# A 31-tap depthwise convolution moved to TensorE as 128x32 products over four-token stacks, and attention values as column halves

## The reference

```python
for l in range(2):
    h = rmsnorm(x, g_mix[l]); p = h @ w_in[l]            # 384 | 256 | 32 | 512 | 512 columns
    q = rmsnorm(c_q) @ w_uq[l]                           # 8 heads of 64 (nope) + 32 (rope)
    kv = rmsnorm(c_kv) @ w_ukv[l]                        # 8 heads of 64 (key) + 64 (value)
    o = softmax(q k^T * scale) @ v                       # per head, 512 x 512
    u = a * sigmoid(gt)                                  # 512 channels
    u[t, ch] = b[ch] + sum_k w_dw_conv[k, ch] * u[t + k - 15, ch]     # k in 0..30
    u = silu(layernorm(u))
    x = x + concat(o, u) @ w_o[l]
    z = dwconv3(rmsnorm(x) @ w_up[l]); x = x + (silu(zg) * zv) @ w_down[l]
return rmsnorm(x, g_final)
```

## Time and profile before

| | before |
|---|---|
| median of 3 runs | 2043.75 us |
| lowest, highest | 2043.48, 2044.87 us |
| the profiled execution | 2043.99 us |
| its span (first to last record) | 2042.3 us |
| mean granted TensorE clock, share of full | 0.988 |
| TensorE busy | 1952.7 us, 96% of the span |
| VectorE busy | 1195.6 us, 59% |
| ScalarE busy | 958.1 us, 47% |
| GpSimd busy | 147.2 us, 7% |

### The profile page before, as it was taken

One profiled execution on the slowest core, in us unless ns is written; L12 is line 12 of the kernel. 1 busy time (PEld: TensorE's weight loads), 2 busy tenths in 40 slices (PEclk: granted clock), 3 DMA queues, 4 the chain that ended last, 5 costly groups with the idle time before them and its releaser, 6 DMA issues.

```text
span 2042.3 us, 25795 instructions
## 1 busy us (share of the span) xinstructions
PE 1952.7 (96%) x8419; PEld 1540.2 (75%) x8419; DVE 1195.6 (59%) x1960; ACT 958.1 (47%) x1722; POOL 147.2 (7%) x148
## 2 busy tenths in 40 slices
PE   8999989799999988999999999999999999999997
PEld 6777778578888866765678888887766578888886
DVE  4555446643343346888566666436698757656534
ACT  4655563343443333477553444334377554434432
POOL 2111000100000003220010000003120010000000
PEclk9999989899999999999999999999999999999998
DMA  4222213133332222221123333333221033333322
GB/s 136 62 64 68 70 54 104 42 94 96 98 98 94 96 78 63 62 37 37 47 83 103 98 89 106 95 96 88 67 43 42 22 95 92 92 103 93 102 94 82
DMA packets 163423, 162.44 MB, mean 80 GB/s; under 512 B 46840, under 2 KB 121550, under 8 KB 163340
## 3 DMA queue, kind: packets, MB, share of 16 engines
q1 hardware_dynamic: 163236, 161.36, 27.1%
q10 hardware_dynamic: 104, 0.03, 0.0%
HBM read 159.24 MB, written 2.10 MB: 79 GB/s over the span
## 4 chain that ended last, share of the span: by engine, by line
PE 88%; DVE 6%; ACT 3%; issue 1%; POOL 1%; DMA 0%; SPq 0%; DVEq 0%; ACTq 0%; POOLq 0%
PE bank_b L2062 15%; PE bank_b L2064 15%; PE bank_b L2063 15%; PE bank_a L2062 12%; PE bank_a L2064 12%; PE bank_a L2063 12%; PE bank_b L2353 3%; PE bank_b L2451 2%; PE bank_a L2164 1%; PE bank_a L2437 1%; DVE x_t L1338 1%; DVE arena L1341 1%; DVE w_lo L1338 1%; DVE arena L1338 1%; DVE h_lo L1341 1%
## 5 line engine op out<-in xcount | busy, mean ns | idle before, releaser
L1338 DVE TENSOR_TENSOR w_lo<-w_raw,w_hi 128x512 fp32r<-128x512 f32 (+3 forms) x621 | 428.3, 702 | 611.0 <-ACT w_hi L1053 365.4
L1053 ACT ACTIVATE w_hi<-w_raw 128x512 fp32r<-128x512 f32 (+3 forms) x396 | 233.0, 599 | 441.9 <-PE bank_b L2064 227.8
L2062 PE MATMUL bank_b<-h_hi,w_hi 128*128 128x512 f32 x944 | 371.2, 393 | 7.4 <-DVE var L1356 3.9
L2063 PE MATMUL bank_b<-h_lo,w_hi 128*128 128x512 f32 x944 | 367.9, 390 | 0.0
L2064 PE MATMUL bank_b<-h_hi,w_lo 128*128 128x512 f32 x944 | 367.8, 390 | 0.0
L2062 PE MATMUL bank_a<-h_hi,w_hi 128*128 128x512 f32 x592 | 235.2, 397 | 30.8 <-DVE h_lo L1341 16.3
L771 ACT ACTIVATE w_hi<-w_raw 128x512 fp32r<-128x512 f32 x225 | 137.8, 629 | 259.4 <-PE bank_b L2064 138.5
L1341 DVE SCALAR_TENSOR_TENSOR arena<-arena,cols_all 128x512 f32<-128x512 f32 x350 | 244.9, 750 | 0.1
L2063 PE MATMUL bank_a<-h_lo,w_hi 128*128 128x512 f32 x592 | 233.1, 394 | 0.0
L2064 PE MATMUL bank_a<-h_hi,w_lo 128*128 128x512 f32 x592 | 233.0, 394 | 0.0
L2062 PEld LDWEIGHTS bank_b<-h_hi,w_hi 128*128 128x128 f32 x944 | 177.5, 188 | 49.0 <-issue 5.0
(11 more groups left out here) (262 smaller groups left out, 2495.9 us busy)
## 6 DMA issues: line engine op xcount, KB each, us to landing
w_raw<-in_w_up_dram SPq DMA_DIRECT2D x240, 256.0 KB, 3.0
w_raw<-in_w_down_dram SPq DMA_DIRECT2D x152, 256.0 KB, 2.5
w_raw<-in_w_in_dram SPq DMA_DIRECT2D x64, 128.0 KB, 2.3
w_raw<-in_w_gate_dram SPq DMA_DIRECT2D x32, 256.0 KB, 2.9
w_raw<-in_w_in_dram SPq DMA_DIRECT2D x32, 256.0 KB, 2.6
w_raw<-in_w_o_dram SPq DMA_DIRECT2D x32, 256.0 KB, 2.6
w_raw<-in_w_out_dram SPq DMA_DIRECT2D x16, 256.0 KB, 2.6
w_raw<-in_w_in_dram SPq DMA_DIRECT2D x16, 192.0 KB, 2.3
```

The costliest lines, as they stand in the source:

```text
L1053: nc.scalar.activation(w_hi[:, s, 0:c], w_raw[:, s, 0:c], ACT.Copy).then_inc(w_round, 1)
L1338: return nc.vector.tensor_tensor(out_, a, b, op)
L2062: nc.tensor.matmul(out_, a_hi, b_hi, start=start, stop=False, skip_group_check=loose)
L2063: nc.tensor.matmul(out_, a_hi, b_lo, start=False, stop=False, skip_group_check=loose)
```

## The change

**Taps.** All 31 taps move to TensorE. A channel tile's 128 partitions are cut into four lanes of 32 channels. For lane c, `stacks[..][:, c, :]` holds on its 128 partitions four copies of the 32 channels, shifted by 0, 1, 2 and 3 tokens. It is made by `stack_up(j)`: 16 transfers within SBUF for each tile, each 32 rows of 540 fp32 numbers, issued by ScalarE. There are two such stacks, used in turn. A product of a 128x32 matrix with 512 columns of a stack then applies four taps to 32 channels, and 8 groups (`GROUPS`) of four such products, one for each lane, make up the 31 taps. The four write different quarters of the partitions of one bank. GpSimd makes the matrices, one operation for each group. `base(j)` adds the bias, and nothing is left to join. VectorE's `taps()` go.

**Values.** `vv` becomes compact (64 columns a head). `values2(j)` does one pair and one block of 128 queries: 8 products of 64 columns out over 128 moving columns, the two heads alternating, into the lower and the upper half of the partitions. It runs in every second step. The steps go through blocks first and heads second, `PV_LAG` becomes 6, and `pts` a ring of eight.

**Order.** The taps of tile 0 move from the middle of `M_KV` to the fifth `M_Q` chunk. The taps of `w_dw_conv` are loaded in 8 pieces a layer, by SyncE, in place of one.

```diff
-PE_TAPS = 8
-DVE_TAPS = CONV_K - PE_TAPS
+SHIFTS = 4
+GROUPS = -(-CONV_K // SHIFTS)
+LANES = P // SHIFTS
+STACK = S + SHIFTS * (GROUPS - 1)
-EXP_LAG, TURN_LAG, PV_LAG = 2, 4, 8
+EXP_LAG, TURN_LAG, PV_LAG = 2, 4, 6
...
@@ transfers of the taps (SyncE)
-                sp_.dma_start(rows_tap[n], w_dw_conv[n]).then_inc(rows2_land, 16)
+                for g in range(GROUPS):
...
+                    sp_.dma_start(rows_tap[n][g * rows:g * rows + rows, 0:(k1 - k0) * LANES].rearrange("q (s c) -> q s c", c=LANES),
+                                  w_dw_conv[n, k0:k1, :].rearrange("s (q c) -> q s c", c=LANES)).then_inc(rows2_land, 16)
...
@@ diagonals (GpSimd)
-                        nc.gpsimd.tensor_scalar(diag[:, r, :], ident[:, :], cols_all[:, l, c:c + 1], None,
+                        nc.gpsimd.tensor_tensor(diag[:, r, :].rearrange("p (c m) -> p c m", c=SHIFTS), taps,
+                                                lanes[:, :].unsqueeze(1).broadcast_to((P, SHIFTS, LANES)),
                                                 ALU.mult).then_inc(diag_made, 1)
...
@@ ScalarE
+                def stack_up(j):
+
+                    act.wait_ge(pad_zero, was[pad_zero.name] + 2)
+                    act.wait_ge(u_ready, was[u_ready.name] + (1, HT, HT, HT)[j])
+                    if j >= 2:
+                        act.wait_ge(diag_used, was[diag_used.name] + (j - 1) * GROUPS)
+                    for c in range(4):
+                        for s in range(SHIFTS):
+                            act.dma_start(stacks[j % 2][s * LANES:s * LANES + LANES, c, :],
+                                          upad[c * LANES:c * LANES + LANES, j, s:s + STACK]).then_inc(stack_land[j % 2], 16)
+
+                for k in range(4, 6):
                     split2(M_KV + k)
-                split2(M_Q)
-
-                act.wait_ge(diag_used, was[diag_used.name] + PE_TAPS)
-                nc.scalar.activation(conv_odd[1], conv_banks[0], ACT.Copy).then_inc(conv_base, 1)
-                for k in range(1, 4):
+                stack_up(0)
+                for k in range(6, KT):
+                    split2(M_KV + k)
+                stack_up(1)
+                for k in range(4):
                     split2(M_Q + k)
...
                 split2(M_PAIR + 1)
+                base(0)
+                stack_up(2)
                 act.wait_ge(sq_added, added0 + KT - 1 + KVT - 1)
...
                     if g == 0:
                         base(1)
+                        stack_up(3)
                         copy_key(1, 0)
...
@@ TensorE
-                def conv_taps(j, taps):
-
-                    for r in taps:
+                def conv_taps(j, groups):
+
+                    for r in groups:
                         if r == 0:
-                            pe.wait_ge(u_ready, was[u_ready.name] + j + 1)
-                            pe.wait_ge(pad_zero, was[pad_zero.name] + 2)
-                        pe.wait_ge(diag_made, was[diag_made.name] + j * PE_TAPS + r + 1)
-                        nc.tensor.matmul(conv_banks[j], diag[:, r, :], upad[:, j, DVE_TAPS + r:DVE_TAPS + r + S],
-                                         start=r == 0, stop=r == PE_TAPS - 1).then_inc(diag_used, 1)
+                            pe.wait_ge(stack_land[j % 2], stacked(l, j))
+                        pe.wait_ge(diag_made, was[diag_made.name] + j * GROUPS + r + 1)
+                        for c in range(4):
+                            rows = slice(c * LANES, c * LANES + LANES)
+                            last = nc.tensor.matmul(conv_banks[j][rows, :], diag[:, r, rows],
+                                                    stacks[j % 2][:, c, SHIFTS * r:SHIFTS * r + S],
+                                                    start=r == 0, stop=r == GROUPS - 1)
+                        last.then_inc(diag_used, 1)
...
-                def values2(n):
...
-                    part = nc.tensor.matmul(bank_b[:, i % 2, :], vv[:, kb, i, hd * P:hd * P + P], pts[hd][:, kb, :],
-                                            start=hd == 0 and kb == 0, stop=hd == 1 and kb == TT - 1)
...
+                def values2(j):
+
+                    i, b = j // TT, j % TT
+                    c = slice(b * P, b * P + P)
...
+                    for kb in range(TT):
+                        for hd in range(2):
+                            rows = slice(hd * ND, hd * ND + ND)
+                            last = nc.tensor.matmul(bank_b[rows, i % 2, c], vv[:, kb, i, rows],
+                                                    pts[(2 * j + hd) % len(pts)][:, kb * P:kb * P + P],
+                                                    start=kb == 0, stop=kb == TT - 1)
+                    last.then_inc(pv_done, 1)
...
-                        values2(g - PV_LAG)
+                    if g >= PV_LAG and (g - PV_LAG) % 2:
+                        values2((g - PV_LAG) // 2)
```

More of the change, by code:

```diff
@@ L316, in two_blocks @@
         gf = arena[:, 9:13, :]
-        CPAD = S + 2 * HALO
-        upad = arena_flat[:, 13 * S:13 * S + 4 * CPAD].rearrange("p (j n) -> p j n", j=4)
-        conv = arena[:, 18:22, :]
-        conv_odd = (arena[:, 22, :], arena[:, 29, :])
-        diag = arena_flat[:, 30 * S:32 * S].rearrange("p (r n) -> p r n", r=PE_TAPS)
-        vv = arena_flat[:, 5 * S:13 * S].rearrange("p (k i n) -> p k i n", k=TT, i=PAIRS)
+        CPAD = STACK + SHIFTS
+        upad0 = 13 * S + S // 4
+        upad = arena_flat[:, upad0:upad0 + 4 * CPAD].rearrange("p (j n) -> p j n", j=4)
+        conv = upad[:, :, 0:S]
+        stacks = [arena_flat[:, first:first + 4 * STACK].rearrange("p (c n) -> p c n", c=4) for first in (18 * S, 9 * S)]
+        diag = arena_flat[:, 30 * S:32 * S].rearrange("p (r n) -> p r n", r=GROUPS)
+        vv = arena_flat[:, 5 * S:9 * S].rearrange("p (k i n) -> p k i n", k=TT, i=PAIRS)
         prob = arena[:, 23:27, :]
@@ L331, in two_blocks @@
         lat_hi, lat_lo = split[:, 0:5, :], split[:, 5:10, :]
-        pts = (arena[:, 0:4, :], sq[:, :, :])
+        pts = [arena[:, n, :] for n in range(4)] + [sq[:, n, :] for n in range(4)]
         kq_hi, kq_lo = ([[h[:, 2 * q + hd, :] for hd in range(2)] for q in range(2)] for h in (h_hi, h_lo))
@@ L486, in two_blocks @@
         vv_ready = sem("vv_ready")
[L487 removed]
         pt_ready = sem("pt_ready")
         pv_done = sem("pv_done")
[L490 removed]
+        tap_zero = sem("tap_zero")
+        stack_land = [sem(f"stack_land{b}") for b in range(2)]
         diag_made = sem("diag_made")
         diag_used = sem("diag_used")
[L493 to L494 removed]
         conv_ready = sem("conv_ready")
@@ L675, in _ @@
                                          base=-P, pattern=[[1, 2 * P]], channel_multiplier=-1))
+            for c in range(P // LANES - 1):
+                made(nc.gpsimd.tensor_tensor(lanes[:, :], (lanes if c else ident)[:, 0:LANES],
+                                             ident[:, (c + 1) * LANES:(c + 2) * LANES], ALU.add))
             def add_squares(count, before_sq, before_add, before_stat):
@@ L1428, in first_normed @@
                                         ALU.mult).then_inc(xn_first, 1)
+            for rows in rows_tap:
+                nc.vector.memset(rows[P - LANES:P, P - LANES:P], 0.0).then_inc(tap_zero, 1)
             dve.wait_ge(cols_made, 1)
@@ L1810, in _ @@
                 for k in range(6, KT):
                     split2_lo(M_KV + k)
-                    taps(2)
-                split2_lo(M_Q)
-                taps(10)
-                for k in range(1, 4):
+                for k in range(4):
                     split2_lo(M_Q + k)
-                    taps(1)
                 dve.wait_ge(w_used, was[w_used.name] + M_KV + KT)
@@ L1837, in rstd_after @@
                     stt(var[:, :], bank, 1.0 / width, epsv, ALU.mult, ALU.add).then_inc(var_ready, 1)
-                    beside()
+                    if beside is not None:
+                        beside()
                     dve.wait_ge(guess_ready, number)
@@ L1906, in _ @@
                     split2_lo(M_PAIR + SLOTS + m)
-                first_taps = tap
                 for g in range(BLOCKS + TURN_LAG):
@@ L1934, in _ @@
                             split2_lo(M_PAIR + (i + 2) * SLOTS + (2, 4, 5, 6).index(m))
-                    if m == 1 and 2 <= i:
-                        dve.wait_ge(o_round, was[o_round.name] + i - 1)
-                        rest(o2_lo[:, i - 2, :], bank_b[:, i % 2, :], o2_hi[:, i - 2, :]).then_inc(o_split, 1)
-                    taps(taps_by(g, first_taps) - tap)
+                    if m == 7 and 1 <= i:
+                        dve.wait_ge(o_round, was[o_round.name] + i)
+                        rest(o2_lo[:, i - 1, :], bank_b[:, (i - 1) % 2, :], o2_hi[:, i - 1, :]).then_inc(o_split, 1)
                 dve.wait_ge(o_round, was[o_round.name] + HT)
@@ L2373, in _ @@
                         total(bank_a[:, 3, :], added0 + KT - 1 + KVT - 1)
+                    if k == 4:
+                        conv_taps(0, range(GROUPS))
```

142 lines of the change are left out of this document (45 added, 97 removed).

## The result

The changed kernel takes 2101.2 us (median of 4 runs, 2100.12 to 2102.16), the kernel before in the same session 2043.62 us: a ratio of 1.0281, 95% interval 1.0263 to 1.0299. It is slower by 57.6 us; 2075 was forecast, with a range of 2037 to 2132.

A forecast was written before the change was run, and what follows sets the result against it. TensorE, busy 96% of the span, was taken as the bound, level with VectorE and ScalarE in late attention steps. Terms -6.7 + 6.0 + 14.9 + 3.6 - 2.0 = +15.8 us a layer, 31.6 for two: 2075 us, range 2037 to 2132.

The forecast's parts named there:

- Taps on TensorE: Tap products: four 32-column products run side by side in 0.86 us, as one product did; cost 0.
- steps: Rival for the taps: quarters overlap only beside a product's second record, +22.4 us a layer, 2120 us; chance 0.17.
- no overlap: Rival for the taps: small products never run side by side, some +80 us a layer, 2235 us; chance 0.14.
- Values: Value products in attention steps: smaller products, two heads at once, save 6.7 us a layer; bounds 0 and -13.7.
- switches: TensorE entering and leaving bursts of small products: 30 uncovered switches at 0.2 us, +6.0 us a layer; bounds 0 and 10.
- The stacks: ScalarE's queue: 16 transfers a stack at 0.35 us each delay the work behind them, +14.9 us a layer.
- Clock: TensorE at half rate after long idle, counted once at the sum and half at stack 3: +3.6 us a layer.
- VectorE's relief: 184 tap operations leave VectorE, so its maxima and query work come sooner: -2.0 us a layer; bounds 0 and -5.
- SyncE's tap loads and GpSimd's diagonals: SyncE's 14 further tap loads (4.3 us) and GpSimd's one operation a group: both forecast at no cost.
- faster: Rival: without stalls at ScalarE's queue and their clock, -2.7 us a layer, 2039 us in all; chance 0.13.

The follow-up runs named there:

- the fourth experiment: Changed kernel with a tile's 32 small tap products reordered, all groups of one column quarter before the next quarter: 2163.83 us (1.0593), 62.6 above the changed kernel.
- experiment 5: Kernel before with the change of the values alone (compact values, 64 columns out, PV_LAG 6), taps as before: 2040.26 us (0.9985), beside 2043.65.
- experiment 6: Kernel before with 20 of VectorE's 23 tap operations of each channel tile left out, nothing else changed: 2035.26 us (0.9964), beside 2043.65.
- the second experiment: Changed kernel with GpSimd in place of ScalarE issuing the 16 transfers of each stack: 2038.05 us (0.9975), beside 2043.26.
- the seventh experiment: Version with GpSimd issuing the stacks, and the scaling of probabilities moved from ScalarE to VectorE: 2025.85 us (0.9916), beside 2043.65.

## Why the prediction was right, and where it was off

It was right in direction, inside its range, and right on the mechanism: ScalarE's issuing holds back what stands behind it. The size was short by almost half of the rise (31.6 forecast, 57.6 measured). By its own steps, a layer:

- **Taps on TensorE, 0.** Right. Four small products take what one took, 0.86 us to the next group. The two rivals against it, steps (2120) and no overlap (2235), fell, and the fourth experiment shows what there is to lose when the order is changed. The estimate from the Trainium skill ("TensorE: Matmul & The Clock Gate", "Part 3: Packing small matmuls — row/col tiling") of 1.08 us a group doesn't hold for four quarters here: 0.86. The same section of the Trainium skill has matmuls start and end strictly in program order. The portions of the fourth experiment don't: their records start out of that order, 16 of them in 1.94 us, and the measurement decides.
- **Values, -6.7, and switches, +6.0.** The size of the burst was about right (its records span 1.09 us, 0.9 was forecast, 1.72 was the price of the two products before), and so was entering and leaving. From one portion of taps to the next it is 2.76 us (905.75 to 908.51); in the kernel before it was 2.41, by the rows below. That is 0.35 for both, 0.2 each forecast. The values alone brought 1.7 us a layer (experiment 5: 3.4 for both). What was misjudged is how much of it ScalarE lets through: 7.9 us a layer less work, and 5 more of waits.
- **The stacks, +14.9.** The step that was mis-sized. The four places were the right ones and so was the order in which work is held. But an issue takes 0.65 us, not 0.35 (its record 0.61, the median of 128), and 0.60 was given as the upper bound, from a row that was ScalarE's first. The idle time is 23.2 us a layer. By place, in the first later layer: 4.78 + 3.88 = 8.66 at stacks 0 and 1, for 3.3 forecast; 8.0 at stack 2, for 6.2; 6.69 at stack 3, for 5.4. A second error hides part of the first: 16 issues of 0.65 are 10.4 us, and at stacks 2 and 3 the forecast let all but 0.2 of a stack reach the path. By that working 11.0 and 10.2 us would have been lost there. Three issues of stack 2 went out beside earlier work of ScalarE, and at stack 3 TensorE still had work for 7 us, from 904.38 to 911.3. Without this, which is luck, the forecast would have been short by some 6.5 us a layer more.
- **Clock, +3.6.** Too small, 8.4 us. More idle times are followed by half-rate products than the two that were counted: four in the first later layer, even behind 3.88 us, and three in the second, while one of 2.71 us in the kernel before had none in the window behind it.
- **VectorE's relief, -2.0.** Too small by half: 4.2 us a layer (experiment 6), with 20 of 23 taps left out. The row of the costliest group gives 244.9 / 350 = 0.70 us of busy time a tap, and not the 0.75 that one lasts, which is most of what the forecast fall of 138 us had too much.
- **SyncE's tap loads and GpSimd's diagonals** at no cost: no run takes them apart, so this isn't shown.

The rows of the kernel before behind the 2.41 us:

```profile
882.67 1.88 PE L2353 MATMUL bank_b<-arena 128*128 128x512 f32 x4
...
885.08 1.88 PE L2353 MATMUL bank_b<-arena 128*128 128x512 f32 x4
```

Together the rise is 28.8 us a layer: +31.6 for stacks and clock, and -2.8 for all the rest (2038.05 against 2043.26 in one session is -2.6). The rest was forecast at -2.7. So the rival "faster", 2039 us without the stalls, is about what the second experiment then measured, 2038.05. That the rest came out so near is luck, as its parts shifted and cancelled. The values brought -1.7 in place of -6.7 and the relief -4.2 in place of -2.0. If the two simply add up, which no run shows, they leave +3.3 for entering and leaving the taps, where +6.0 was forecast for all switches. The rows would give eight portions at 0.35 and two whole tiles at 0.24 (from the first of their products to the second behind them it is now 867.76 - 860.42 = 7.34 us, before 838.02 - 830.92 = 7.10), 3.3 too.

## What to carry to other kernels

Before a transfer goes onto a compute engine's queue, multiply its issues by the price of one and look at what stands behind them: here 16 small transfers held ScalarE for 10 us, whatever they moved, and the same transfers on the queue of GpSimd, which had time to spare, turned +2.8% into -0.25%. When work leaves an engine that wasn't the bound, look at once for what can move in, since that is where the gain is (0.6% more here, from an edit that alone costs 0.7%). And a product for a quarter of the columns is free only beside those for the other quarters: interleave them. Two in a row for one quarter still cost nothing here, eight in a row cost three times the time.

## What the runs showed of the hardware

- Four 128x32 fp32 products in different column quarters over 512 columns take 0.86 us together, as one of 128x128; eight in a row in each quarter, quarter after quarter, took 22.6 us for 32. With two in a row the trace has products of later quarters starting ahead of their turn in the queue.
- A transfer within SBUF costs its issuer 0.65 us on ScalarE (10.33 us for 16), 0.60 on SyncE (2.40 for 4) and 0.51 on GpSimd (8.09 for 16), from one issue to the next. On ScalarE 8 or 32 rows and 270 or 540 numbers a row made no difference; the other two weren't tried with other sizes.
- The length of an idle time doesn't settle alone whether the granted clock falls: behind 2.71 us there was none of it in the kernel before, and none behind 3.33 us in the changed kernel's second later layer, but with SyncE's issues behind 2.71 us there was (the sum at 844.48 took 2.08 in place of 1.02 us, and the granted clock from 844 to 848 was 0.50). Behind 3.88 us the slow products came 1.6 us after the first ones.
- In the attention steps, scaling 128x512 numbers keeps VectorE 0.40 us from its next operation (942.85 to 943.25 in the seventh experiment), where ScalarE needs 0.61 (965.02 to 965.63 in the kernel before). The records last 0.49 and 0.71 us.
